# Fewer VectorE rows between the units of the second attention group, more of them beside two runs of weight slabs

## What is computed

```python
proj = x @ w_in                       # q | k | v | u
att  = rms_norm(band_attention(q, k, v))      # 16 heads x 64
ssm  = rms_norm(s5(u))                        # complex-diagonal state space, GELU, gate
x1   = layer_norm(ALPHA * x + concat(att, ssm) @ w_out)
# PEER: product-key retrieval over 128*128 single-neuron experts
q = x1 @ wq ; s = q . keys ; top 16 of each half, then top 16 of the 256 sums, 8 heads
a   = sum_d x1[t] * u_tab[idx[t, k]]          # 128 experts a token
hid = gelu(a) * softmax(top scores)
y   = sum_k hid[t, k] * v_tab[idx[t, k]]
x2  = layer_norm(ALPHA * x1 + y)
```

## Time and profile before

| | |
|---|---|
| median of 3 runs | 4036.3 us (4023.76 to 4037.44) |
| the profiled execution | 4029.4 us, of which 4027.6 us are the span |
| TensorE matmul busy | 2640.9 us (66%) |
| VectorE busy | 2808.7 us (70%) |
| ScalarE busy | 344.4 us (9%) |
| GpSimd busy | 1267.5 us (31%) |
| mean granted TensorE clock | 0.773 of full speed |
| HBM traffic | 1334.3 MB, mean 331 GB/s |

### The profile page before, as it was taken

How to read it: one execution, slowest core, us unless ns; L and a number is a source line. 1 busy time by engine, 2 the same in 40 slices (tenths; PEclk the granted TensorE clock), 3 DMA queues, 4 the chain that set the end, 5 groups by cost and what they waited for, 6 DMA issues and landing times.

```text
span 4027.6 us, 31038 instructions
## 1 busy us (share of the span) xinstructions
PE 2640.9 (66%) x11464; PEld 2022.3 (50%) x11464; DVE 2808.7 (70%) x3301; ACT 344.4 (9%) x805; POOL 1267.5 (31%) x1386
## 2 busy tenths in 40 slices
PE   6989889986799576695989899999977000000000
PEld 6869567943475344453558777777766000000000
DVE  4350121077976888777779868997656989999888
ACT  0110221100001222101010000000000000000000
POOL 1450000012212222222222222222222367777772
PEclk8985569997769555797999999999999555555555
DMA  7663235579878899897999999999999999999997
GB/s 223 224 190 98 63 128 167 178 222 393 289 274 297 343 336 370 359 421 289 422 389 421 423 423 423 423 423 422 423 378 416 348 349 397 409 410 383 395 375 332
DMA packets 291063, 1334.30 MB, mean 331 GB/s; under 512 B 69536, under 2 KB 129472, under 8 KB 139488
## 3 DMA queue, kind: packets, MB, share of 16 engines
q0 software_dynamic: 140432, 952.56, 59.4%
q1 hardware_dynamic: 110384, 365.54, 24.4%
q10 hardware_dynamic: 40096, 14.22, 1.8%
HBM read 1284.43 MB, written 57.20 MB: 333 GB/s over the span
## 4 chain that ended last, share of the span: by engine, by line
PE 33%; DMA 29%; DVE 23%; POOL 7%; issue 7%; ACTq 1%; ACT 1%; SPq 0%; DVEq 0%; POOLq 0%
PE low L1446 20%; DMA arena<-in_peer_v,arena 15%; DMA arena<-in_peer_u,arena 6%; DVE arena L1262 6%; DVE acc L1275 6%; POOL arena L590 4%; DMA arena<-in_w 3%; POOL arena L581 3%; PE low L1550 2%; DMA arena<-g_scratch 2%; DMA arena<-bias_scratch 2%; PE acc L1509 1%; PE low L1509 1%; PE low L1534 1%; DVE low L1275 1%
## 5 line engine op out<-in xcount | busy, mean ns | idle before, releaser
L1275 DVE SCALAR_TENSOR_TENSOR acc<-arena,acc 128x2048 f32<-128x2048 f32 x443 | 1042.9, 2354 | 303.3 <-DMA arena<-in_peer_v,arena 260.8
L1446 PE MATMUL low<-arena 128*128 128x192 f32 (+1 forms) x4096 | 1050.3, 419 | 60.7 <-DMA arena<-in_w 44.5
L1759 PE MATMUL low<-arena 128*128 128x256 f32 x4096 | 916.6, 383 | 115.1 <-DMA arena<-in_ut 113.7
L1446 PEld LDWEIGHTS low<-arena 128*128 128x128 f32 x4096 | 747.8, 197 | 349.3 <-DMA arena<-in_w 40.0
L1759 PEld LDWEIGHTS low<-arena 128*128 128x128 f32 x4096 | 773.2, 191 | 258.2 <-DMA arena<-in_ut 140.9
L581 POOL DMA_INDIRECT arena<-in_peer_v,arena x576 | 573.6, 996 | 958.7 <-DVE acc L1275 807.9
L1262 DVE SCALAR_TENSOR_TENSOR arena<-arena,acc 128x2048 f32<-128x2048 f32 x320 | 725.6, 2285 | 125.9 <-DMA arena<-in_peer_u,arena 119.9
L581 POOL DMA_INDIRECT arena<-in_peer_u,arena x320 | 320.1, 1000 | 1382.6 <-DVE arena L1262 899.6
L1275 DVE SCALAR_TENSOR_TENSOR low<-arena,low 128x2048 f32<-128x2048 f32 x126 | 296.6, 2354 | 29.4 <-DMA arena<-in_peer_v,arena 14.4
L590 POOL DMA_INDIRECT arena<-expert_scratch,arena x256 | 262.2, 1024 | 79.4 <-issue 79.1
L1550 PE MATMUL low<-arena 128*128 128x128 f32 x320 | 87.7, 437 | 94.7 <-DVE arena L1112 87.1
(11 more groups left out here) (265 smaller groups left out, 1949.5 us busy)
## 6 DMA issues: line engine op xcount, KB each, us to landing
arena<-in_w SPq DMA_DIRECT2D x128, 1024.0 KB
arena<-in_ut SPq DMA_DIRECT2D x128, 1024.0 KB
expert_scratch<-arena SPq DMA_DIRECT2D x128, 128.0 KB
arena<-bias_scratch SPq DMA_DIRECT2D x16, 640.0 KB, 5.8
arena<-in_peer_v,arena POOLq DMA_INDIRECT x576
arena<-toeplitz_scratch SPq DMA_DIRECT2D x64, 128.0 KB
arena<-c_scratch SPq DMA_DIRECT2D x64, 128.0 KB
bias_scratch<-distance_scratch POOLq DMA_DIRECT2D x1, 5120.0 KB, 26.1
```

The costliest lines, as they stand in the source:

```text
L1275: stt(held, slot[j], wv_, held, ALU.mult, ALU.add).then_inc(used, 1)
L1446: ins = mm(L[n % 2][:, 0:width], wring[n % 2][:, k, :], rhs(k), start=k == 0, stop=k == KT - 1)
L1759: ins = mm(L[j % 4][:, 0:NSD], ud[j % 4][:, k, :], lane(catB, k)[:, P:NB], start=k == 0, stop=k == KT - 1)
```

## The change

In the loop over group B's units the second `rows()`, behind `back(u)`, is taken out: VectorE does 48 rows there, not 96. Both `rows(50)` become `rows(62)`. That places 24 of the 48 rows left out; the other 24 have no call of their own and fall to `rows_to(R_U2 + 4)`, behind the decode of tile 2, which now does 54 rows and not 30. All 896 rows are still done, in the same order. On ScalarE the GELU of part 0 moves from unit 30 to unit 40.

```diff
@@ -900,7 +900,7 @@
                 if v == 4:
                     gates(1)
-                if v == 30:
+                if v == 40:
                     activated(0)
@@ -1379,7 +1379,6 @@
                     front(u + 1)
                 rows()
                 back(u)
-                rows()
                 if v == 8:
                     gate(0)
@@ -1392,11 +1391,11 @@
             link(ins)
             dve.sem_inc(cat_ready, 1)
             link.zero()
-            rows(50)
+            rows(62)
             for t in range(NGA, NT):
                 ln1(t, x1s[t], x1s[t], lngB, lnbB, low, rows)
                 rows(2)
-            rows(50)
+            rows(62)
             dve.wait_ge(keys_in, 48)
```

## The result

The changed kernel takes 4142.9 us (median of 4 runs, 4133.4 to 4146.7) against 4032.0 for the kernel before (4 runs, 4023.8 to 4037.4; the 4036.3 us of the table above is the median of three of them): ratio 1.0258, 95% interval 1.0236 to 1.028, slower. The profiled execution took 4141.1 us, of which 4139.3 are the span.

What follows compares the result with a forecast made beforehand. Bound taken: mainly bytes over bandwidth from 1669 us on; in the attention, VectorE's loop with TensorE. From the profiled 4029.4 us, - 2 + 16 + 89.6 - 7 gave 4126 us, +2.4%; range 4055 to 4153.

Steps and rivals of the forecast that it cites:

- The bound of the attention: Group B's attention: the row taken out is covered by TensorE's turn and scores, so the loop does not shorten; -2 us.
- The small terms inside the -2: Attention: four high-clock units and some smaller ones gain about 0.4 us each; bounds -8 and +6 us.
- the forecast's upper bound: Attention: spells of high clock shift away with the new timing, +6 us.
- The price of a row: Outside the attention a moved row costs its transfer, 2.49 us at 421 GB/s; bounds 2.36 and 2.7 us.
- the dearer price: At the skill's 358 GB/s a row would cost 2.93 us, making the sum 16 us higher.
- The mix stage: Mix slabs: 12 more rows and ScalarE's wait for row 191 overlap and don't add; +16 us, bounds 11 and 21.
- The other 36 rows: Query slabs to row 640: 12 rows beside query slabs, 24 behind tile 2's decode, each costing its transfer; +89.6 us.
- the 7 us of filled idle time: From 2070.4 to 2090 us, DMA share 0.64: moved rows use idle DMA time; -7 us, bounds -7 and 0.
- The sum: Whole kernel: 4029.4 - 2 + 16 + 89.6 - 7 = 4126 us, +2.4%; bounds 4110 and 4153.
- (a): Attention: the row taken out sets the unit, 113 us saved, total 4015 us; chance 0.05.
- (b): Slab and expert stages: moved rows hide in VectorE's idle time, total 4027 us, no change; chance 0.07.
- (c): Attention: TensorE's clock rises, 67 us less if held for all 48 units, total 4059 us; chance 0.13.

Runs made afterwards that it cites:

- The two swaps: back(u) moved ahead of the rows: in the kernel before, both rows kept, ratio 0.9872; in the changed kernel, one row, ratio 0.9907 to before.
- the run with 24 rows: Kernel before with the second row of every other attention unit taken out, both rows(50) kept: ratio 1.0132.
- runs without bytes: Changed kernel with 24 of the 128 table slabs of the expert products loaded to a sixteenth: median 4080.5 us, ratio 1.0124 to before.
- without VectorE's work: Changed kernel with VectorE's instruction for rows 262 to 639 over 1024 of 2048 columns, all gathers kept: ratio 1.0226 to before.
- stall alone: Changed kernel with both rows(62) set back to rows(50), ScalarE's wait for row 191 kept: median 4172.4 us, ratio 1.0337 to before.
- rows alone: Changed kernel with ScalarE's GELU of part 1 moved behind the copies of all 16 mix slabs, 62 rows kept: ratio 1.0245 to before.
- the swapped one: Changed kernel with back(u) moved ahead of its one row: median 3998.4 us, ratio 0.9907 to before.
- in turn: Changed kernel with back(u) ahead of one or two rows a unit alternately, rows(62) twice: median 3999.2 us, ratio 0.9913 to before.

## Why the prediction was right, point by point

**The bound of the attention.** Right: -2 forecast, +0.8 measured, and the waits for scores rose to 149.2 us where 151 were forecast. The small terms inside the -2 did not come as written. Before, four spells of the high clock had units of 5.16 and 5.36 us; the changed kernel has one such spell, with units of 4.76 and 5.02. The gain of 0.4 us in a fast unit is there, but most fast units are gone, which is the case of the forecast's upper bound. From the first front to the last the stage is 3.5 us longer, and behind the last front, where one row fewer stands, 2.8 us shorter. That the two nearly cancel was not foreseen. The two swaps show which row was on the loop: the same 48 rows, placed on the other side of `back(u)`, take 131 us off, 106 of them by the row and the rest, as far as it can be told, by the clock.

**The price of a row.** Right in size: 2.58 us in the run with 24 rows and 2.49 with 48. The runs without bytes (-55.6 us) and without VectorE's work (-14.7 us for 400 us) show that it is the transfer. Where it is paid was wrong: the forecast had the moved rows land in stages with DMA at 1.01 and 1.02, but beside the expert products nothing changed (252 rows for 254, 1014.9 us for 1018.3), and 33 of the 36 rows came out behind them, at a share of 0.94 in the mean. The plain rows there still come at 2.46 us, with the share at 1.01; the mean is lower because of the LayerNorms and the last rows in that part. So 2.49 held there too, but the reason given for it was that of another stage.
The Trainium skill's figure of 358 GB/s for the HBM side ("DMA: Bandwidth & Descriptors", section "Where 436 GB/s comes from") was named in the forecast as the dearer price. This case's trace disagrees: the changed kernel's stages beside slabs and products held 415 to 421 GB/s, and the measured 82.0 us agree with 2.49 us a row.

**The mix stage.** The mechanism was right in both halves: 35.9 us of ScalarE for 34, 17.8 us of TensorE for 16, and two paths that end together. The size was +18.3 for +16, inside its bounds of 11 and 21. What the forecast couldn't show, that they don't add, the runs did: stall alone 202.8, rows alone 202.4, both 201.8.

**The other 36 rows.** +82.0 for +82.6, the 7 us of filled idle time among it. ScalarE's later GELUs made no stall: row 447 was done at 2779.9 us (2783 forecast), part 2 ran at 2839.1 (2827 forecast), and ScalarE did not wait for it.

**The sum.** 4126 against a median of 4142.9 and a profile of 4141.1. The stages make +101.3 us, against 96.6 forecast (-2 + 16 + 89.6 - 7); the other 10.3 us of the profile lie ahead of the attention. So 4.7 of the 15 us between forecast and profile are errors of its terms, and 10.3 are that execution's. That the time ahead of the attention moves by up to 17 us between executions was no term of my range.

**The rivals.** (a), the row sets the unit, fell with the attention's length. (b), moved rows hide, fell with the two runs that took bytes and work away. About 7 us of it are true, where the DMA share was below 1, and so is the part of the 12 rows beside the mix slabs that went into VectorE's wait there. (c), the clock rises, did not happen in the changed kernel (0.52, after 0.55 before), but it is real one step further on: with the loop's own row out of it, TensorE was busy 160 of 195 us and the clock stood at 0.82. The Trainium skill ("TensorE: Matmul & The Clock Gate", Part 1) has activity as what releases the clock. These runs fit it only in part: in the changed kernel TensorE was busy 224 of 313 us and the clock stayed low, in the swapped one 160 of 195 and it rose; but with both rows behind the diagonal it was busy 220 of 270 us, the same share of the time as in the swapped one, and the clock stayed at 0.53.

## What to carry to other kernels

Before taking work off a busy engine, find which side of its handshake the work stands on: here one of two equal instructions lay beside TensorE's turn and cost nothing, the other lay between a result that had arrived and the answer that TensorE waited for, and cost 2.2 us in every unit; putting the answer first gained 1.3%, taking the wrong one out lost 2.6%. Where the DMA share is at 1, an engine's idle time is not room, and work that brings its own transfer costs bytes over bandwidth; in a fixed order of work the cost can show in a later stage than the one it was moved to, so compare stages cut at the same events, not windows of time. Removing it from a stage pays only if that stage then gets shorter by more than the transfers that leave it.

## What the runs showed of the hardware that was not expected

The clock in the swapped loops. One row behind the diagonal had TensorE at a mean of 0.82 and units of 3.8 us in the mean (3.0 to 3.5 in most at the high clock); two rows had it at 0.53 and units of 5.2 to 5.7 in most; in turn, 0.57. TensorE's pause before a turn does not tell the two apart: 0.4 to 0.95 us in the fast units, and under 0.8 us in 20 of the 34 slow ones of two rows that had a pause of over 0.3. Whether the clock rises because units are short or the other way round, these runs don't tell.

The last stretch, rows 640 to 895 with two gathers of different kinds in turn, took 692.6 to 702.2 us in twelve profiles and 677.4 and 677.1 in the two taken on one other chip, where the kernel before was faster too, 4021.6 us against 4032.0 to 4038.5. So some 17 us of this kernel's time differ from chip to chip in that stretch. The traces show where: GpSimd's 474 gather instructions of that stretch took 455 us in both profiles of that chip and 479 to 491 in the twelve others, 0.96 us each and not 1.01 to 1.03. Why they do was not tried.
